# Remainders of eight weight chunks on GpSimd, layer-norm sums added on VectorE, one key join earlier, and idle products on TensorE

## The reference, cut to what matters

```
h = rms_norm(x, mix_norm_g)
q, kv, gate_logits, conv_in = split(h @ w_in)
conv = silu(layer_norm(causal_depthwise_conv(a * sigmoid(gate), 31 taps)))   # 1024 channels
attn = nsa_attention(q, kv, sigmoid(gate_logits), ...)
x = x + concat(attn, conv) @ w_out
x = x + (silu(g) * a) @ w_down    # (a, g) = conv3(rms_norm(x, ffn_norm_g) @ w_up)
x = rms_norm(x, final_norm_g)
```

## Time and profile before

| | |
|---|---|
| median of 3 runs | 2220.71 us |
| the profiled execution, its own time | 2220.59 us |
| its span, first to last instruction | 2218.8 us |
| TensorE busy | 2188.2 us |
| VectorE busy | 1574.1 us |
| ScalarE busy | 1123.3 us |
| GpSimd busy | 128.3 us |
| bytes read | 499.54 MB |

### The profile page before, as it was taken

The page is one execution under the profiler, slowest core; times in us unless marked ns, Lnnn a source line. Parts: engine busy times, 40 slices in busy tenths (PEclk is TensorE's granted clock), DMA queues, the critical chain, the costliest instruction groups (busy, mean ns, idle before and its releaser), DMA issues.

```text
span 2218.8 us, 29547 instructions
## 1 busy us (share of the span) xinstructions
PE 2188.2 (99%) x11637; PEld 1853.1 (84%) x11637; DVE 1574.1 (71%) x2417; ACT 1123.3 (51%) x1683; POOL 128.3 (6%) x92
## 2 busy tenths in 40 slices
PE   7999999999999999999999999999999999999998
PEld 6888787888888888888889887878888888888986
DVE  5896886899998799998875665576555555544455
ACT  5444775555543455554455656554444444444443
POOL 5850000000000000000000000000000000000000
PEclk9999999999999999999999999999999999999999
DMA  7754436788899888889955551647676776655563
GB/s 265 225 190 149 135 99 207 245 291 286 292 313 369 308 281 289 290 286 373 338 169 180 177 175 55 233 140 248 230 221 227 227 233 233 214 192 189 182 214 118
DMA packets 139915, 504.00 MB, mean 227 GB/s; under 512 B 15616, under 2 KB 18048, under 8 KB 138880
## 3 DMA queue, kind: packets, MB, share of 16 engines
q1 hardware_dynamic: 138960, 496.85, 67.0%
q0 software_dynamic: 528, 3.16, 0.4%
q10 hardware_dynamic: 288, 2.10, 0.3%
HBM read 499.54 MB, written 2.51 MB: 226 GB/s over the span
## 4 chain that ended last, share of the span: by engine, by line
PE 84%; DVE 12%; ACT 2%; issue 1%; DMA 0%; POOL 0%; POOLq 0%; SPq 0%; DVEq 0%; ACTq 0%
PE bank L627 20%; PE both L627 18%; PE bank L617 13%; PE bank L630 10%; PE both L630 9%; PE bank L618 7%; DVE w_lo L1675 5%; DVE raw L1657 2%; PE bank L620 1%; PE bank L622 1%; PE bank L621 1%; ACT ffn_g L1403 1%; ACT ffn_a L1397 1%; PE bank L876 1%; PE both L833 1%
## 5 line engine op out<-in xcount | busy, mean ns | idle before, releaser
L1675 DVE TENSOR_TENSOR w_lo<-raw,w_hi 128x1024 fp32r<-128x1024 f32 x693 | 840.7, 1222 | 449.7 <-ACT w_hi L1193 448.3
L1193 ACT ACTIVATE w_hi<-raw 128x1024 fp32r<-128x1024 f32 x737 | 767.7, 1054 | 616.2 <-PE bank L630 295.2
L617 PE MATMUL bank<-h_both,w_hi 128*128 128x512 f32 x1936 | 495.0, 395 | 2.8 <-DVE h_both L1732 2.8
L617 PEld LDWEIGHTS bank<-h_both,w_hi 128*128 128x128 f32 x1936 | 346.1, 189 | 66.0 <-DVE h_both L1732 4.4
L618 PEld LDWEIGHTS bank<-h_both,w_lo 128*128 128x128 f32 x1936 | 264.7, 190 | 19.1
L618 PE MATMUL bank<-h_both,w_lo 128*128 128x256 f32 x1936 | 272.2, 283 | 0.0
L1657 DVE SCALAR_TENSOR_TENSOR raw<-raw,silu_c 128x1024 f32<-128x1024 f32 x192 | 234.0, 1219 | 0.0
L627 PE MATMUL bank<-w_hi,h_both 128*128 128x512 f32 (+2 forms) x1024 | 233.9, 372 | 0.0
L627 PE MATMUL both<-w_hi,h_both 128*128 128x512 f32 (+1 forms) x960 | 228.4, 379 | 1.4 <-DVE h_both L1752 1.4
L627 PEld LDWEIGHTS bank<-w_hi,h_both 128*128 128x128 f32 x1024 | 181.9, 188 | 33.1 <-issue 0.7
L627 PEld LDWEIGHTS both<-w_hi,h_both 128*128 128x128 f32 x960 | 169.3, 188 | 33.9 <-DVE h_both L1752 2.8
(11 more groups left out here) (369 smaller groups left out, 2343.9 us busy)
## 6 DMA issues: line engine op xcount, KB each, us to landing
raw<-weights SPq DMA_DIRECT2D x924, 512.0 KB, 4.5
raw<-weights SPq DMA_DIRECT2D x5, 504.0 KB, 7.3
x<-x SPq DMA_DIRECT2D x2, 1024.0 KB, 5.8
bias<-bias_rows SPq DMA_DIRECT2D x8, 256.0 KB, 6.8
silu_c<-c ACTq DMA_DIRECT2D x2, 1024.0 KB, 4.7
gate_row<-gate_rows POOLq DMA_DIRECT2D x2, 1024.0 KB, 9.0
out<-x SPq DMA_DIRECT2D x8, 256.0 KB, 2.7
final_row<-final_row POOLq DMA_DIRECT2D x1, 1024.0 KB, 5.2
```

Source lines behind the costliest of these rows:

```text
L617: return e.matmul(out, hi, a_both[:, k, :, :].rearrange("p a t -> p (a t)"), start=first, stop=last)
L1193: e.activation(w_hi[:, n % PART_SLOTS, 0:widths[i]], raw[:, i % RAW_SLOTS, 0:widths[i]], ACT.Copy).then_inc(hi_ready, 1)
L1675: e.tensor_tensor(w_lo[:, slot, 0:widths[i]], raw[:, i % RAW_SLOTS, 0:widths[i]], w_hi[:, slot, 0:widths[i]].bitcast(F32), ALU.subtract).t ...
```

## The change

The plan puts the four chunks of `conv_first` on GpSimd too, and of the first feed-forward the split chunks 1 to 4 (counted from 0 at `up_first`; the fifth chunk in line is an `ada` chunk, so the last of the four is the first chunk of `up_a` 1). GpSimd's program is set for that: it does the remainders up to the end of the attention's output product, then the two powers, then those four remainders, and only then waits for the feed-forward.

For the layer norm VectorE adds the eight tiles of conv_y into one (`ln_q`), two at a time behind each pair of convolved tiles, and later the eight tiles of squares; TensorE makes one product with ones for each sum instead of eight. The last key tile (2,1) is split and joined before the two engines go through the three chunks past it. TensorE makes 18 products on a zeroed tile before the first turn (8 once VectorE has zeroed the tile, 10 once x has landed), 5 more between the first two turns, and 2 before the first weight product.

```
+    p.pool_rate = 1.0
     p.project_pair("conv_first", ("conv_a", 0), ("conv_g", 0), "w_in", (conv, conv + CONV_CH), P)
-    p.pool_rate = 1.0
...
+            p.to_pool_next = range(1, 5)
             p.project_pair("up_first", ("up_a", 0), ("up_g", 0), "w_up", (0, DFF), P)
...
+        WARM_PRODUCTS = (8, 10)
+        IDLE_PRODUCTS = ((5, 2), (10, 0), (15, 5), (17, 4))
-        IDLE_PRODUCTS = ((0, 0), (10, 0), (15, 5), (17, 4))
...
+            w.wait_ge(dve_step, 1)
+            keep_busy(0, WARM_PRODUCTS[0])
+            w.wait_ge(x_landed[0], 16)
+            keep_busy(0, WARM_PRODUCTS[1])
             w.wait_ge(gains_landed, 16)
...
+            def norm_sum(added, taken):
+                w.wait_ge(norm_added, added)
+                fill(7)
+                e.matmul(banks[7][:, 0:T], ones, ln_q[:, :], start=True, stop=True).then_inc(ln_summed, 1)
+                free[7] = taken, 1
...
-            fill(7)
-            for j in range(CONV_TILES):
-                w.wait_ge(taps_done, j + 1)
-                t = e.matmul(banks[7][:, 0:T], ones, conv_y[:, j, :], start=j == 0, stop=j == CONV_TILES - 1)
-            t.then_inc(ln_summed, 1)
-            free[7] = ln_mean_ready, 1
+            norm_sum(1, ln_mean_ready)
```

The second sum changes in the same way (`norm_sum(2, ln_var_ready)`). In ScalarE's program, the last key tile:

```
+                if at_key == 2:
+                    round_until(final["key", br, j])
+                    w.wait_ge(multiplied, done_at["key", br, j])
+                    split_low(banks[bank_of["key", br, j]], 32, (keys_ready, 2))
+                    round_until(lead(final["key", br, j]))
```

In VectorE's program, the additions to the sum of conv_y, `join_scaled`, and the additions of the squares; in GpSimd's, the chunks ahead of the powers:

```
+                    w.wait_ge(dve_step, last_tap[j0 + 1])
+                    if j0 == 0:
+                        so_far_y = chain(e.tensor_tensor(ln_q[:, :], conv_y[:, 0, :], conv_y[:, 1, :], ALU.add))
+                        yield
+                        continue
+                    for j in (j0, j0 + 1):
+                        w.wait_ge(dve_step, so_far_y)
+                        t = e.tensor_tensor(ln_q[:, :], ln_q[:, :], conv_y[:, j, :], ALU.add)
...
-                rests_until(lead(final[key]))
+                rests_until(lead(final[key]) if i < 32 else final[key])
...
+            rests_until(lead(final["key", 1, 0]) + 1)
+            w.wait_ge(squared, 2)
+            t = chain(e.tensor_tensor(ln_q[:, :], ln_sq[:, 0, :], ln_sq[:, 1, :], ALU.add))
+            for j in range(2, CONV_TILES):
+                w.wait_ge(squared, j + 1)
+                w.wait_ge(dve_step, t)
+                if j < CONV_TILES - 1:
+                    t = chain(e.tensor_tensor(ln_q[:, :], ln_q[:, :], ln_sq[:, j, :], ALU.add))
+                else:
+                    e.tensor_tensor(ln_q[:, :], ln_q[:, :], ln_sq[:, j, :], ALU.add).then_inc(norm_added, 1)
...
-            rests_until(lead(final["out_attn", 3]))
+            rests_until(final["out_attn", 3])
...
+            rests_until(c_first - 1)
             w.wait_ge(ff_ready, FF_TILES)
```

More of the change, by code:

```diff
@@ L84, in __init__ @@
         self.pool_due = 0.0
+        self.to_pool_next = ()
+        self.started = 0
         self.open = False
@@ L106, in piece @@
             self.new_chunk("split")
+            if self.to_pool_next:
+                if self.started in self.to_pool_next:
+                    self.on_pool.add(len(self.chunks) - 1)
+                self.started += 1
+                if self.started == self.to_pool_next[-1] + 1:
+                    self.to_pool_next = ()
             self.pool_due += self.pool_rate
@@ L432, in two_blocks @@
         low = place("low", "mid", 0, [P, 2, T])
+        blank = place("blank", FR, 0, [P, 512], BF16)
         sig = place("sig", "mid", (KD + KD // 2) * T * 4 + 2048, [P, 2, T])
@@ L696, in keep_busy @@
                 if number:
-                    src = (None, mix_hi, ff_hi, mix_hi)[stage]
-                    b = (None, 5, 2, 2)[stage]
+                    b = (2, 5, 2, 2)[stage]
                     fill(b)
                     for _ in range(number):
-                        e.matmul(banks[b][:, :], src[:, 0, 0:P], src[:, 0:2, :].rearrange("p k t -> p (k t)"), start=True, stop=True)
+                        if stage == 0:
+                            e.matmul(banks[b][:, :], blank[:, 0:P], blank[:, :], start=True, stop=True)
+                        else:
+                            src = (mix_hi, ff_hi, mix_hi)[stage - 1]
+                            e.matmul(banks[b][:, :], src[:, 0, 0:P], src[:, 0:2, :].rearrange("p k t -> p (k t)"), start=True, stop=True)
             def turn_steps(stage, freed):
@@ L807, in tensor_program @@
                 free[2 + tt] = gates_ready, tt + 1
-            fill(7)
-            for j in range(CONV_TILES):
-                w.wait_ge(taps_done, j + 1)
-                t = e.matmul(banks[7][:, 0:T], ones, conv_y[:, j, :], start=j == 0, stop=j == CONV_TILES - 1)
-            t.then_inc(ln_summed, 1)
-            free[7] = ln_mean_ready, 1
+            norm_sum(1, ln_mean_ready)
             for at_key, (br, j) in enumerate(((1, 1), (2, 0), (2, 1))):
                 if at_key == 1:
-                    fill(7)
-                    for i in range(CONV_TILES):
-                        w.wait_ge(squared, i + 1)
-                        t = e.matmul(banks[7][:, 0:T], ones, ln_sq[:, i, :], start=i == 0, stop=i == CONV_TILES - 1)
-                    t.then_inc(ln_summed, 1)
-                    free[7] = ln_var_ready, 1
+                    norm_sum(2, ln_var_ready)
                 wide_tile(("key", br, j), need, (keys_ready, at_key + 2))
@@ L1301, in scalar_program @@
             for at_key, (br, j) in enumerate(((1, 1), (2, 0), (2, 1))):
-                split_low(made(("key", br, j)), 30 + at_key, ((low_joined, 21), (keys_ready, 1), (keys_ready, 2))[at_key])
+                if at_key == 2:
[3 more added lines that the diff above has]
+                    round_until(lead(final["key", br, j]))
+                else:
+                    split_low(made(("key", br, j)), 30 + at_key, ((low_joined, 21), (keys_ready, 1))[at_key])
                 if at_key == 0:
@@ L1775, in conv_taps @@
             def conv_taps():
-                before = {}
+                before, last_tap = {}, {}
                 for j0 in range(0, CONV_TILES, 2):
@@ L1795, in conv_taps @@
                                 w.wait_ge(dve_step, before[j])
-                                e.scalar_tensor_tensor(conv_y[:, j, :], u, tap_w, so_far, ALU.mult, ALU.add).then_inc(taps_done, 1)
+                                last_tap[j] = chain(e.scalar_tensor_tensor(conv_y[:, j, :], u, tap_w, so_far, ALU.mult, ALU.add))
                             yield
+                    w.wait_ge(dve_step, last_tap[j0 + 1])
[7 more added lines that the diff above has]
+                        if j < CONV_TILES - 1:
+                            so_far_y = chain(t)
+                        else:
+                            t.then_inc(norm_added, 1)
+                        yield
             tapping = conv_taps()
@@ L1919, in vector_program @@
             join_scaled(("key", 2, 1), 32, keys[:, 1, 1, :], 1.0, keys_ready)
+            rests_until(lead(final["key", 2, 1]))
             for j in range(CONV_TILES):
```

10 lines of the change are left out of this document (6 added, 4 removed).

## The result

The changed kernel takes 2228.85 us (median; 2227.59 to 2229.09), the kernel before in the same comparison 2220.57 (2220.49 to 2220.9). The ratio is 1.0035, 95% interval 1.0025 to 1.0045: 8.3 us slower, outside the range of 2212.4 to 2220.6. The profiled execution took 2228.79, its span is 2227.0, against 2218.8: 8.2 more.

What follows compares the result with a forecast made beforehand. TensorE was taken as the bound, busy 2188.2 of 2218.8 us. Start 2.9 - 0.3, layer norm 1.5 and feed-forward 1.8 - 0.3 sum to 5.6 us gained, so 2215.0; range 2212.4 to 2220.6.

Steps and rivals of the forecast that it cites:

- Does GpSimd hold VectorE up?: Start and feed-forward: GpSimd's remainders meeting VectorE's scalings cost 0.3 us at each place, within bounds 0 and 2.41 per meeting.
- The rival of the whole remainder: Start and feed-forward: GpSimd holds the port for its whole remainder; start gains 1.4, feed-forward loses 1.1; 2218.8 us; chance 0.24.
- The slower rival: Scalings at start and feed-forward: GpSimd's remainders slip between back-to-back scalings, costing 2.41 each time; five make 2226.5 us; chance 0.08.
- The clock at the start: Start: idle products leave TensorE's clock at its upper level before the turns, removing the slow pace of the first products.
- two things: Start, first product to ninth step: 2.3 us above undisturbed pace, made of slow-clock products and waiting for h_lo behind remainders.
- The first weight product: Start: without the first remainder on VectorE, TensorE's first weight product comes 0.9 us earlier, at 13.3 instead of 14.16.
- 0.9 + 2.3 - 0.3: Start: earlier first product, plus slow pace and h_lo waits removed, less ScalarE's pacing; a gain of 2.9 us.
- The layer norm: Layer norm with keys: single-product sums, a 3.9 us wait for the second, 1.4 at the value chunk; net gain 1.5 us.
- the clock rival: Idle products fail to lift the clock before the turns, or it falls in the norm's 3.9 us wait; 2216.5; chance 0.12.
- GpSimd's pace: Start and feed-forward: a remainder takes GpSimd 2.41 us against VectorE's 1.22, yet none is late for TensorE.
- The feed-forward: First feed-forward: VectorE loses three remainders, TensorE's waits of 0.68 and 0.66 go; gain 1.8 us before 0.3 for contact.

Runs made afterwards that it cites:

- both_back: The changed kernel with all eight remainders (start and first feed-forward) given back to VectorE; 2220.58 us, ratio 1.0000 to the kernel before.
- meet: The kernel before plus, behind its last store, phases timing VectorE and ScalarE instructions alone and beside GpSimd remainders; profiled once, no kernel time compared.
- all_apart: norm_filled with second and fourth remainders of start and feed-forward on GpSimd, held until scalings finish, and the value chunk's remainder before the last key's join; 2217.11 us.
- norm_filled: both_back with 16 idle products on TensorE ahead of the layer norm's second sum; 2219.01 us, ratio 0.9993 to the kernel before.
- cold_start: norm_filled without the idle products at the start (the 18 and the 7 between the turns); 2219.19 us, ratio 0.9993 to the kernel before.
- start_back: The changed kernel with only the four remainders at the start given back to VectorE; 2225.17 us, ratio 1.0019 to the kernel before.
- disturb: The kernel before with three GpSimd additions that feed nobody, behind the powers at the first feed-forward's start; 2222.69 us, ratio 1.0009.

## Why the prediction was wrong

**The step that failed** is "Does GpSimd hold VectorE up?", where a meeting was priced at 0.3 each place, "the delay of the earlier trace rows, the nearest row". That row has the other direction: a power of 0.19 that waits for a scaling. The wait is as long as the rest of the other engine's instruction, so it should have been turned round with the length of the remainder, 2.4. Measured: two scalings held at the start by 2.1 each and one by 1.3, in the feed-forward the pairs 2.1 and 3.2 longer, and a remainder by 1.4. With the clock that fell behind these waits the eight remainders cost 8.3 us (both_back against the changed kernel).

The second error is in the count of meetings. The step names quarters 2 and 3 as the places at the start, but by its own numbers the first remainder runs from 11.4 while VectorE scales until 12.58: the largest delay, twice 2.1, lies in those first three scalings. The rival of the whole remainder (0.24, 2218.8) had the price right and let each remainder be met once. The slower rival (0.08, 2226.5) had them slip between scalings, and it is what happened; against it stood that two scalings start 0.40 apart and last 0.48. The overlap in the records doesn't keep GpSimd out: in meet it got in between scalings that stood just so. That its 2226.5 stands near 2228.85 is in part luck: it took off 6.2 for a gain without contact that no kernel here reached (all_apart, which holds four of the eight apart, gains 3.6), added 12.1 where the five delays of scalings above make 10.8, and left out the clock (1.5 in the feed-forward alone).

**The clock at the start**: the idle products lift it (in norm_filled's trace it fell again before the turns), but what they lift is not on the path. With them and without them the ninth step starts at 23.84 (both_back) and 23.83 (cold_start). The "two things" of the step, the slow pace and the wait for h_lo, were not to be added: TensorE's slow pace lay under its wait for h_lo, and a term for it should have been 0.

**The first weight product** at 13.3 and the rest of "0.9 + 2.3 - 0.3" could not come with the contact; two remainders of the start on GpSimd, held apart, gave 0.7. What all four could give is not shown.

**The layer norm** was right in each of its steps: the wait is 4.04 (3.9 forecast), the new wait at the value chunk 1.22 (1.4), the one at the keys is gone, and with the clock held up the scores start 1.27 earlier than before (229.49 in norm_filled; 1.5 forecast). What it lacked is the clock rival's second half, "it falls in the new wait of 3.9 us", priced at 1.5 and measured at 1.6. The price was taken from the slow pair of the start, another place, so that it fits is in part luck. It had 0.12 as part of a rival that also held the idle products' failure; the two are separate events, and this one came true. The Trainium skill (TensorE: Matmul & The Clock Gate, "Why this matters for your kernels") warns of such gaps; the trace agrees: 4.04 idle, then 1.41 for a pair of 0.81.

**GpSimd's pace** was right: no product waits for one of its remainders, not even in the changed kernel. **The feed-forward**: the waits of 0.68 and 0.66 became 0 and 1.88, and a new one of 2.54 stands ahead of the first turns. The 1.8 supposed no contact; two remainders held apart there gave 0.7.

## What to carry to other kernels

Before work is moved from VectorE to GpSimd, list VectorE's instructions that will run beside it, and charge those whose operands all lie in SBUF with up to the whole length of GpSimd's instruction, once for each instruction in GpSimd's row; the forms with an operand in PSUM that were measured here cost nothing. With half of GpSimd's instructions held back by a semaphore until the scalings were done, the same move paid a little (0.7 us). A saving that leaves TensorE waiting some 4 us for another engine should be priced with the clock that it loses, and idle products in the wait keep it; a lifted clock is worth nothing where another engine sets the pace.

## What was not expected of the hardware

In meet GpSimd and VectorE alternated strictly, instruction by instruction, while both had work from and to SBUF: eight scalings beside three remainders took some 9.5 us instead of 3.3. The Trainium skill (SBUF — State Buffer, "SBUF: two separate sides") has a lock held for the whole instruction, and names the case of two SBUF inputs, too; the traces agree with both (2.6 for a scaling, 3.44 for two additions). What it doesn't say is who comes next when both have more to do, and that is what made the difference between 2218.8 and 2226.5 here. Of the time that VectorE's row shows in such a stretch most is waiting: the profile counts it as busy (5.48 for three scalings), so it stands in no list of idle time, and shows only as the mean duration of a group.

After 3.97 us of idleness at the start and 4.04 in the norm the clock was at its lower level. After 2.54 in the feed-forward it wasn't in the changed kernel (0.73 for the pair at 390.34), but behind the wait of 1.88 it fell, at 398. In start_back's trace it fell soon after the same 2.54 (at 387.69), and in disturb it was down after waits of 1.61 and 0.96 (1.22 for the pair at 386.44). So shorter waits than 4 us can bring it down, and not in every execution; what decides it, these runs leave open.
